# Router product with its weights stationary in four column groups, and one more product that adds the partial sums

## The reference

```python
def hier_moe(h, w_group, b_group, w_expert, b_expert, w_gate, w_up, w_down):
    t = h.reshape(-1, d)
    group_prob = jax.nn.softmax((t @ w_group).astype(f32) + b_group.astype(f32), axis=-1)
    gp, gi = lax.top_k(group_prob, 1)
    exp_logits = ((t @ w_expert).astype(f32) + b_expert.astype(f32)).reshape(-1, MOE_GROUPS, MOE_EXPERTS_PER_GROUP)
    in_group = jnp.einsum('tg,tge->te', jax.nn.one_hot(gi[:, 0], MOE_GROUPS, dtype=f32), exp_logits)
    ev, ei = lax.top_k(in_group, MOE_TOP_K)
...
    h = h + mixed @ w_out[layer]
    h = h + hier_moe(rms_norm(h, norm_ffn_g[layer]), moe_w_group[layer], ...)
```

## Time and profile before

| | us |
|---|---|
| median of three runs | 1238.91 |
| lowest and highest of them | 1237.07, 1241.5 |
| span of the profiled execution, first to last instruction | 1240.9 |
| PE busy | 1111.8 (90%) |
| DVE busy | 832.5 (67%) |
| ACT busy | 624.6 (50%) |
| POOL busy | 448.6 (36%) |
| PE busy at L1737, the router product, 128 records | 16.2 |

### The profile page before, as it was taken

How to read it: one execution, slowest core, us unless ns; L and a number is a source line. 1 busy time by engine, 2 the same in 40 slices (tenths; PEclk the granted TensorE clock), 3 DMA queues, 4 the chain that set the end, 5 groups by cost and what they waited for, 6 DMA issues and landing times.

```text
span 1240.9 us, 21691 instructions
## 1 busy us (share of the span) xinstructions
PE 1111.8 (90%) x7030; PEld 886.4 (71%) x7030; DVE 832.5 (67%) x1211; ACT 624.6 (50%) x979; POOL 448.6 (36%) x291
## 2 busy tenths in 40 slices
PE   5899899999978879999999928999999899999994
PEld 4898799999967545555565516887877687877872
DVE  4797647453467455544344187898887989888986
ACT  5522111156432354434343225787776787877863
POOL 1130211122000101110012122787866686977960
PEclk9999999999988979999899958999999999999998
DMA  7216213232044440011111575589799888776444
GB/s 254 93 32 88 67 61 89 63 98 69 20 90 104 171 156 1 18 52 34 49 54 68 175 282 186 182 285 348 239 385 368 292 271 259 255 263 193 121 150 162
DMA packets 85157, 190.73 MB, mean 154 GB/s; under 512 B 7745, under 2 KB 27713, under 8 KB 84433
## 3 DMA queue, kind: packets, MB, share of 16 engines
q1 hardware_dynamic: 78464, 165.69, 38.8%
q0 software_dynamic: 6624, 24.12, 8.3%
HBM read 220.61 MB, written 31.51 MB: 203 GB/s over the span
## 4 chain that ended last, share of the span: by engine, by line
PE 66%; DVE 14%; ACT 7%; DMA 5%; issue 4%; POOL 2%; SPq 1%; ACTq 0%; POOLq 0%; DVEq 0%
PE ps L2172 24%; PE ps L452 11%; PE ps L1750 9%; PE ps L1723 3%; PE ps L1700 3%; DVE split L2270 2%; ACT split L2218 2%; PE ps L2152 2%; PE ps L1381 1%; PE ps L464 1%; POOL split L2115 1%; DMA weights<-in_w_up 1%; PE ps L1717 1%; PE ps L1737 1%; DMA mem<-in_final_norm_g 1%
## 5 line engine op out<-in xcount | busy, mean ns | idle before, releaser
L2172 PE MATMUL ps<-split 128*128 128x512 f32 x1728 | 416.4, 396 | 21.7 <-DVE split L2270 13.4
L2172 PEld LDWEIGHTS ps<-split 128*128 128x128 f32 x1728 | 320.0, 189 | 99.9 <-DVE split L2270 21.2
L2218 ACT CAST split<-weights 128x1024 fp32r (+1 forms) x288 | 297.8, 1052 | 109.3 <-PE ps L2172 89.0
L2270 DVE TENSOR_TENSOR split<-weights,split 128x1024 fp32r<-128x1024 f32 x216 | 303.7, 1459 | 50.4 <-ACT split L2218 49.9
L452 PE MATMUL ps<-xsplit,wsplit 128*128 128x384 f32 (+2 forms) x1440 | 250.7, 329 | 0.0
L2115 POOL TENSOR_TENSOR split<-weights,split 128x1024 fp32r<-128x1024 f32 x72 | 199.2, 2767 | 107.3 <-ACT split L2218 106.5
L452 PEld LDWEIGHTS ps<-xsplit,wsplit 128*128 128x128 f32 x1440 | 228.2, 190 | 6.0 <-issue 1.4
L238 POOL TENSOR_TENSOR wsplit<-mem,wsplit 128x1024 fp32r<-128x1024 f32 x22 | 55.0, 2501 | 262.2 <-ACT wsplit L307 262.2
L1750 PE MATMUL ps<-mem 128*128 128x512 f32 x256 | 119.1, 610 | 0.7 <-DVE mem L1587 0.7
L1559 DVE TENSOR_REDUCE sml<-ps 128x1 f32<-128x1040 f32 (+7 forms) x64 | 46.5, 768 | 84.6 <-PE ps L1700 84.6
L1643 ACT COPY mem<-ps 128x512 f32<-128x512 f32 (+3 forms) x48 | 21.4, 481 | 135.0 <-PE ps L1717 89.3
(11 more groups left out here) (413 smaller groups left out, 1422.7 us busy)
## 6 DMA issues: line engine op xcount, KB each, us to landing
weights<-in_w_down SPq DMA_DIRECT2D x26, 2048.0 KB, 16.4
weights<-in_w_gate SPq DMA_DIRECT2D x50, 1024.0 KB
weights<-in_w_up SPq DMA_DIRECT2D x50, 1024.0 KB
mem<-in_w_in SPq DMA_DIRECT2D x22, 512.0 KB, 4.1
mem<-in_x SPq DMA_DIRECT2D x10, 512.0 KB, 3.6
mem<-in_w_out SPq DMA_DIRECT2D x1, 4096.0 KB, 13.2
h_d<-mem SPq DMA_DIRECT2D x8, 512.0 KB, 2.9
xn_d<-mem SPq DMA_DIRECT2D x8, 512.0 KB, 2.6
```

The costliest lines, as they stand in the source:

```text
L2172: mm = nc.tensor.matmul(ps[:, bank + h, :], x, w[place % RING][:, 512 * h:512 * h + 512], start=(k == 0 and p_ == 0), stop=(k == n - 1 and ...
L2218: nc.scalar.copy(WH[place % RING], raw(kind, k, q)).then_inc(wh_ready, 1)
L2270: nc.vector.tensor_tensor(WL[place % RING], raw(kind, k, q), WH[place % RING].bitcast(F32), ALU.subtract).then_inc(wl_dve, 1)
```

## The change

The weight matrix gets 12 columns of zeros, so that it is 32 wide. The router product is turned round: a 128x32 block of `WRT` is stationary and the 128 rows of `XT2` move. Block k goes to column group k % 4 of PE, that is to PSUM partitions 32j to 32j+31, so each group sums two of the eight blocks. ACT copies the 128x128 of partial sums to `RPART`. A new ring item, s, multiplies it in one more matmul by `FOLD` (four 32x32 identities below each other, made once by a DVE reduction of the identity): that adds the four groups and turns the result, and ACT copies its 20 columns to `LGR` as before. Item s of tile p stands in step 4p+15, behind item m if there is one, and in step 40 for the last tile. Three semaphores are merged away to make room for the new one; the mask's load now counts in `akq_loaded`, the gain's in `params_loaded` (where SP first waits for the count 64), and the two routing counts follow on in `gaps_ready`.

```diff
         def sp_hgrn(sp):
-            sp.dma_start(GS, a["subln_g"].to_broadcast([P, P])).then_inc(gains_loaded, 16)
+            sp.wait_ge(params_loaded, 64)
+            sp.dma_start(GS, a["subln_g"].to_broadcast([P, P])).then_inc(params_loaded, 16)
...
-            sp.dma_start(con[:, C_MASK:C_MASK + P], a["consts"][:, C_MASK:C_MASK + P]).then_inc(gains_loaded, 16)
+            sp.dma_start(con[:, C_MASK:C_MASK + P], a["consts"][:, C_MASK:C_MASK + P]).then_inc(akq_loaded, 16)
...
-        GF, WRT, LGR = take(D), take(KD, 20), take(NT, 20)
+        GF, WRT, LGR = take(D), take(KD, 32), take(NT, 20)
+        RPART, FOLD = take(P), take(32)
...
+            ring += [("s", p, None) for p in range(NT) if step_of("s", p) == step]
...
-            nc.gpsimd.tensor_tensor(WRT, WRT, par[:, P_GMIX:P_GMIX + KD].unsqueeze(2).to_broadcast([P, KD, 20]), ALU.mult).then_inc(pool_filled, 1)
+            nc.gpsimd.tensor_tensor(WRT, WRT, par[:, P_GMIX:P_GMIX + KD].unsqueeze(2).to_broadcast([P, KD, 32]), ALU.mult).then_inc(pool_filled, 1)
...
             dve_lambda(dve, link)
+            nc.vector.tensor_reduce(FOLD, ident.rearrange("p (j i) -> p i j", i=32), AX.X, ALU.add).then_inc(fold_ready, 1)
             dve.wait_ge(nlam_ready, 1)
...
+            elif kind == "r":
+                nc.scalar.copy(RPART, b[:, 0:P]).then_inc(ring_free, 1)
             else:
                 nc.scalar.copy(LGR[:, tile_of(n)], b[:, 0:20]).then_inc(ring_free, 1)
...
-            else:
+            elif kind == "r":
                 pe.wait_ge(ring_free, xt_at[n])
                 pe.wait_ge(pool_filled, 5)
                 for k in range(KD):
-                    mm = nc.tensor.matmul(b[:, 0:20], XT2[:, n % 2, k], WRT[:, k], start=(k == 0), stop=(k == KD - 1))
+                    j = k % 4
+                    mm = nc.tensor.matmul(b[32 * j:32 * j + 32, 0:P], WRT[:, k], XT2[:, n % 2, k], start=(k < 4), stop=(k >= 4))
+            else:
+                pe.wait_ge(ring_free, part_at[n])
+                if n == 0:
+                    pe.wait_ge(fold_ready, 1)
+                mm = nc.tensor.matmul(b[:, 0:20], RPART, FOLD[:, 0:20], start=True, stop=True)
```

More of the change, by code:

```diff
@@ L945, in build @@
         MHALF, SQ1 = sml[:, 360:376], sml[:, 376:377]
-        gains_loaded = sem("gains_loaded")
         lb_dve, lb_act = sem("lb_dve"), sem("lb_act")
@@ L1437, in build @@
             sem(n) for n in ("prd_ready", "lam_sum", "lame_ready", "nlam_ready"))
+        fold_ready = sem("fold_ready")
         qk_done, max_ready, exp_done, a_ready, ring_ready, ring_free = (
@@ L1456, in step_of @@
         def step_of(kind, n):
-            return n + {"t": 1, "o": 2}[kind] if kind in "to" else 4 * n + {"m": 7, "x": 13 - 2 * (n == NT - 1), "r": 14 - 2 * (n == NT - 1)}[kind]
+            return n + {"t": 1, "o": 2}[kind] if kind in "to" else 4 * n + {"m": 7, "x": 13 - 2 * (n == NT - 1), "r": 14 - 2 * (n == NT - 1), "s": 15 - 3 * (n == NT - 1)}[kind]
         ring = []
@@ L1466, in build @@
             ring += [("r", p, None) for p in range(NT) if step_of("r", p) == step]
-        at_ready, out_at, mix_at, xt_at = ({n: r + 1 for r, (kind, n, g) in enumerate(ring) if kind == k} for k in "tomx")
+            ring += [("s", p, None) for p in range(NT) if step_of("s", p) == step]
+        at_ready, out_at, mix_at, xt_at, part_at = ({n: r + 1 for r, (kind, n, g) in enumerate(ring) if kind == k} for k in "tomxr")
         def sp_attention(sp):
@@ L1499, in pool_attention @@
             link(nc.gpsimd.memset(HALF, -0.5))
-            pool.wait_ge(gains_loaded, 32)
+            pool.wait_ge(params_loaded, 80)
             link(nc.gpsimd.tensor_scalar(GS8, GS8, 1.0 - LAM_INIT, None, ALU.mult))
             pool.wait_ge(ffn_loaded, 48)
-            nc.gpsimd.tensor_tensor(WRT, WRT, par[:, P_GMIX:P_GMIX + KD].unsqueeze(2).to_broadcast([P, KD, 20]), ALU.mult).then_inc(pool_filled, 1)
+            nc.gpsimd.tensor_tensor(WRT, WRT, par[:, P_GMIX:P_GMIX + KD].unsqueeze(2).to_broadcast([P, KD, 32]), ALU.mult).then_inc(pool_filled, 1)
             for p in range(NT + 1):
@@ L1689, in pe_logits @@
             if n == 0:
-                pe.wait_ge(akq_loaded, 32)
-                pe.wait_ge(gains_loaded, 32)
+                pe.wait_ge(akq_loaded, 48)
             else:
@@ L1786, in build @@
         efree, edown, npair = sml[:, 366:366 + NB].bitcast(I32), sml[:, 334:334 + NB].bitcast(I32), sml[:, 504:505].bitcast(I32)
-        rt_gap, rt_exp, onehot_ready, rank_done, slots_ready, tables_ready, slot_hot_ready, idx_done = (
-            sem(n) for n in ("rt_gap", "rt_exp", "onehot_ready", "rank_done", "slots_ready", "tables_ready", "slot_hot_ready", "idx_done"))
+        rt_exp, onehot_ready, rank_done, slots_ready, tables_ready, slot_hot_ready, idx_done = (
+            sem(n) for n in ("rt_exp", "onehot_ready", "rank_done", "slots_ready", "tables_ready", "slot_hot_ready", "idx_done"))
         def act_route(act, link):
-            act.wait_ge(rt_gap, 1)
+            act.wait_ge(gaps_ready, 3)
             nc.scalar.activation(GX, GX, ACT.Exp).then_inc(rt_exp, 1)
-            act.wait_ge(rt_gap, 2)
+            act.wait_ge(gaps_ready, 4)
             nc.scalar.activation(E2, E2, ACT.Exp).then_inc(rt_exp, 1)
@@ L1846, in dve_route @@
             first_of_max(OHG, gl, GM)
-            tt(GX, gl, b4(GM), ALU.subtract).then_inc(rt_gap, 1)
+            tt(GX, gl, b4(GM), ALU.subtract).then_inc(gaps_ready, 1)
             link(tt(EXO, LG[:, :, 4:20].rearrange("p t (g e) -> p t g e", g=4), OHG.unsqueeze(3).to_broadcast([P, NT, 4, 4]), ALU.mult))
@@ L1852, in dve_route @@
             first_of_max(O2, IG, M2)
-            tt(E2, M2, M1, ALU.subtract).then_inc(rt_gap, 1)
+            tt(E2, M2, M1, ALU.subtract).then_inc(gaps_ready, 1)
             for o, oh in ((OK1, O1), (OK2, O2)):
@@ L2490, in layout @@
     par[:, P_C1:P_C1 + 256], par[:, P_C2:P_C2 + 256] = np.concatenate(c), np.concatenate(c[::-1])
-    router = np.concatenate([g["moe_w_group"][0], g["moe_w_expert"][0]], axis=1)
+    router = np.concatenate([g["moe_w_group"][0], g["moe_w_expert"][0], np.zeros((D, 12), np.float32)], axis=1)
     return {
```

## The result

The changed kernel ran in 1235.36 us (median of 11 runs, 1228.1 to 1240.68), the kernel before beside it in 1241.23 (11 runs, 1236.89 to 1246.99). The ratio is 0.9945, 95% interval [0.9923, 0.9967]: faster by 0.55%, beyond the 0.3% that I had called measurable. I had forecast no change. The time lies inside my range only because that range was wide enough for a rival, and because I had counted from the 1238.91 of three runs: counted from the 1241.23 of eleven, the same range would have begun at 1237.3 and missed it.

A forecast was written before the change was run, and what follows sets the result against it. PE holds 66% of the span, but the first output quarter also waits for DVE's residual sum, which limits the gain. 3.54 - 2.56 - 0.74 = +0.24 us on the median 1238.91 gave 1239.2, range 1235 to 1243.5.

The forecast's parts named there:

- Item s: Folding product ahead of the second output quarter: 3.54 us lost, 1.3 to 1.5 of it work, the rest waiting.
- The floor of DVE: First output quarter behind the router product can't start before DVE's residual pair ends plus 0.14 us; limits gains to 2.56.
- Item r: Router product, 16 passes: 1.81 us now, 0.6 taken after the change, 0.43 if four groups run at once.
- The steps together: Attention steps: 3.54 us lost at the folding product against 2.56 gained at the router product.
- The tail: End of the attention stage: 0.74 us gained, 0.44 from an earlier square and 0.3 at the last tile.
- The half-clock stretch: In tile 1's router product PE's clock fell to 1.2 GHz; priced at 3.3 us, its vanishing only a rival, chance 0.15.
- The sum 3.54 - 2.56 - 0.74: Loss at the folding product less gains at the router product and the stage's end: +0.24 us.
- My second rival: The half-clock stretch in tile 1's router product vanishes, 3.3 us less: 1235.9 us; chance 0.15.
- a new stretch coming: Rival: thinner PE work in steps 15 to 31 brings another half-clock stretch, +3.3 us: 1242.5; chance 0.13.
- What lies behind the stage starts from its end and shifts with it: Part after the attention stage: claimed only to move with the stage's end, no term of its own.
- The slower rival: Column groups don't run side by side, router product 2.0 us: 5.6 us lost in all, 1244.5; chance 0.09.

The follow-up runs named there:

- the profile of after: The changed kernel's profile, against the kernel before; the changed kernel measured 1235.36 us, ratio 0.9945.
- fold one step later: The changed kernel with the folding product one step later (4p+16) for tiles 0 to 5; ratio 0.9952 against the kernel before, steps 225.13 us.
- after's third profile: The changed kernel run once more, unchanged, for a third trace; one run without a ratio, steps 227.27 us, tail 5.96 us.
- the second comparison: The kernel before and the changed kernel both run again unchanged; 1241.04 us and 1234.09 us, ratios 1.0018 and 0.9952.

## Why the prediction was wrong, point by point

- **The floor of DVE: right.** In all r steps the quarter starts 0.14 to 0.15 behind DVE's pair. What PE's busy time seemed to promise went into waiting, as said.
- **Item r, 0.6 us taken: too long, without effect in the steps.** From first to last start it is 0.37 us, on average 0.025 a pass or 0.40 for 16, so four groups run fully side by side, a little under even the lower bound that I had (0.43). The floor hid the error.
- **Item s: right, 3.47 for 3.54.** Its work is 0.24 and the 0.08 in the quarter's first pass, for the 0.35 that I took; the waits for ACT's copy of o are where I put them.
- **The steps together: right**, +0.92 for 3.54 - 2.56 = +0.98.
- **The tail: half right.** 0.25 for 0.74 in the profile of after, where the clock fell to half as the last tile's product began, so that this took 1.14 us:

```profile
717.08 1.08 PE L1743 MATMUL ps<-mem 128*32 128x128 f32 x16
718.22 0.27 ACT L1667 COPY mem<-ps 128x128 f32<-128x128 f32 x1 [1.06 <-PE ps L1743]
718.63 0.59 PE L1748 MATMUL ps<-mem 128*128 128x20 f32 x2 [0.47 <-ACT mem L1667]
719.25 0.18 ACT L1669 COPY mem<-ps 128x20 f32<-128x20 f32 x1 [0.77 <-PE ps L1748]
719.53 0.33 DVE L1854 TENSOR_TENSOR mem<-mem,sml 128x160 f32<-128x160 f32 x1 [0.82 <-ACT mem L1669]
```

  At full clock (fold one step later, after's third profile) it is 5.96, a gain of 0.90: 0.45 ahead of the last product, for the 0.44 forecast, and 0.45 from its start on, for 0.3.
- **The half-clock stretch: the step that failed.** The sum 3.54 - 2.56 - 0.74 has no term for the clock. In its place the runs show 3.4 us in the steps of the profiles, and 3.1 us by the mean clock of the second comparison. My second rival had its place and its price (3.3 us), and I gave it 0.15, as if the stretch were an accident of its place. It fell in the middle of a narrow product, and the change takes all eight of those away. That this is enough the old form with 120 columns moving shows: 3.4 us less in the steps of its profile and 4.1 +- 1.4 in the time, at the same pass time. The row stood in front of me; I read it as a matter of where the work is thin, and gave about as much to a new stretch coming (0.13). No wide form has shown one in the steps.
- **"What lies behind the stage starts from its end and shifts with it": wrong**, in single profiles. A copy of 0.2 us at its head changes one block by 3 us through an order of DVE and POOL. It works in both directions. Whether it is behind the 2 us that are left of the changed kernel's gain stays open, but it should have widened the range.
- **The slower rival: its price right in size** (+5.1 in the steps and +1.0 in the tail for my 5.6 in all), its condition false; where it was made true, the clock hid it in the time.

## What to carry to other kernels

When the granted clock falls in a trace, look at which product it falls in, and whether it does so in other profiles of the same kernel; if the change takes that product away, its cost belongs in the sum before any pricing of passes. A product gains nothing by getting shorter until the engine behind it lets go; here PE's busy time at the product fell by 10.6 us and the steps gained 2.5 by it, and a helper item put where PE never waited cost 3.5. Put such an item where PE waits anyway. And before blaming a part of one profile, multiply the difference of the mean clocks of many runs by the time.

## What the runs showed of the hardware

- Granted clock and moving columns: with 20 moving columns against a 128x128 stationary block PE lost 1.7 to 3.4 us to half clock in seven of eight profiles of this stage, with 120 or 128 in none of nine, at equal busy time. This holds for the steps; ahead of them and in the tail there is half clock in both forms. The old product takes no more time with six times the columns (steps 226.38 against 226.34 at full clock).
- With four column groups which share all 128 rows, four passes start within 0.02 us and the next four 0.11 to 0.13 us behind them: 0.37 us from the first start to the last of 16. In one group every pass starts about 0.11 us behind the one before, 1.86 us until the quarter starts. By the Trainium skill, "TensorE: Matmul & The Clock Gate", Part 3, weight loads overlap running matmuls only where the row group differs. These runs don't agree with it.
- DVE and POOL in one block of the experts: of two differences of 128x1024 that start within 0.03 us of each other, one takes what it takes elsewhere and the other is held back, by 1.1 us (POOL, 3.50 against 2.40) or by 2.2 (DVE, 5.73 for its three against 3.50).
